# A two-layer transformer trunk with routed experts: expert rows added to the residual by accumulating DMAs, the last two experts' rows spread by matmul in both layers, and a closing norm that works by rows

## Chip, cores, metric

The kernel runs on one core of a Trainium2 chip. The metric is the device time of one execution in microseconds. All arithmetic is in 32-bit floats; large products are made of three matmuls over numbers split into a rounded hi part and a lo rest (float32r).

## What is computed

400 token rows of width 1024 (16 meta rows, 256 prompt rows, 8 x 16 decode rows) go through two layers. What matters here is the second half of a layer, after attention:

```python
probs = softmax(x @ router_w)                     # 16 experts in 4 groups
# per token: the best group, the two best experts inside it
gate = probs[chosen two]; gate = gate / sum(gate)
for e in range(16):
    hid = silu(x @ w_gate[e]) * (x @ w_up[e])     # 1024 -> 512
    y = y + combine[:, e] * (hid @ w_down[e])     # combine holds the gates
x = layer_norm(ALPHA * x + y, ln2_g, ln2_b)
```

The result of layer 0 is the input of the next layer's projection (w_in, 2048 columns). The result of layer 1, without the meta rows, is the output.

## The kernel before

**Data.** H holds the residual as rows, four tiles of 128 (tile 3 has the 16 meta rows; layer 1's experts work on tiles 0 to 2 only). FT holds it transposed for the projections, as hi (FThi) and lo (FTlo). ring has six slots of 2 MB for weights, filled by SP's DMAs in a fixed order.

**Experts.** Routing gives each token two seats, (expert, place). POOL gathers up to 128 rows of an expert from the copy xs in DRAM with an indirect DMA (L2131), PE transposes them, and PE multiplies with the gate and up weights (`up`, L930) and with the down weights (`down`, L963). ACT rounds each quarter of the weights (L1810, L1823), DVE subtracts for the lo part (L1342, L1349). Experts go in eight pairs. The result (up to 128 x 1024 in PSUM) is copied by ACT or, for the last but one expert, by DVE into ob (L1840, L1369), and POOL scatters it to the buffer ys in DRAM (L2181), at row token + 400 * k for the token's choice k. PE's order for a pair is written out in `pair` (L1004), ACT's at L1849 and DVE's at L1393. Should an expert have more than 128 tokens, further rounds follow; with these inputs there is one round per layer.

**Gates.** POOL computes each tile's two gates (`share`, L2134), for the last tile after the first gathers and after the residual has been multiplied by ALPHA (`h_prepared`, L2050). PE counts the tokens of each expert (`totals`, L588) at the end of the routing.

**End of layer 0.** All sixteen experts scatter. POOL waits for the scatters (round_closed), then ACT loads both halves of ys for each tile (L2003) and multiplies the first by its gate (`scale_y`, L1655), POOL or DVE adds it to H (`y_summed`, L2057; L1579), DVE multiplies and adds the second (L1583) and takes mean and variance (`ln_front`, L1077). POOL takes the power for rstd (L2047), DVE writes normalized rows z (`ln_z`, L1086), PE transposes them (L555), ACT and DVE apply gain and bias per partition while copying to FT (`turned_h`), ACT rounds (L1643), POOL subtracts (`ft_rest`, L2071). PE's projection in layer 1 starts once all four tiles are rounded (L797). DVE applies gain and bias to the rows in H afterwards (L1104, L1110). SP's loads of w_in into slots 3 and 2 wait until ys has been read; those into slots 0 and 1 don't.

**End of layer 1.** Experts 14 and 15 are not scattered. DVE builds for each a matrix seat x token that holds the gates (`end_gates`, `end_seats`), PE transposes it (L990), ACT copies it to spread, and PE multiplies it in full 32-bit passes with the two results (`end_sums`, L993). The rows of experts 0 to 13 are loaded from ys by SP as soon as expert 13's scatter has landed (L512 to L515), ACT scales the first half between its weight splits (`end_scaled`, L1843), POOL adds it (L2063), DVE the second half (L1442) and PE's sums (L1448). The norm follows by rows, on DVE, ACT and POOL; SP stores each tile (L532).

```python
                if seated and l == END:
                    act.wait_ge(spread_ps, 1)
                    act.activation(spread, PS[:, 2:4, ...], ACT.Copy).then_inc(spread_sb, 1)
                    end_scaled(0)
                split_down(PAIRS - 1, 1, range(1), last=True)
```

## Time and profile before

| | |
|---|---|
| runs, us | 1056.26, 1053.43, 1056.66; median 1056.26 |
| profiled execution, span | 1056.7 us, 15062 instructions |
| PE, DVE, ACT, POOL busy | 91%, 81%, 62%, 26% |
| granted clock, mean | 0.946 |
| DMA | 272.26 MB, mean 258 GB/s |

The profile gives no time for the profiled execution beside its span; the span lies 0.4 us above the median of the runs. Layer 0's experts run from about 215 to 510 us and layer 1's from about 733 to 1031; the attention of each layer lies before them. The time of an instruction is its busy time on its engine. A line can be that of a helper with several callers. In the timeline an engine with a q behind its name (SPq, ACTq) is its queue issuing a DMA.

### The profile page before, as it was taken

How to read it: one execution, taken by the hardware profiler on the slowest of the kernel's cores; microseconds unless marked ns; L12 is line 12 of the kernel's file. 1: busy time of each engine (PE TensorE's matmuls, PEld its weight loads, DVE VectorE, ACT ScalarE, POOL GpSimd, SP SyncE). 2: the span in 40 equal slices, each digit the busy share in tenths (PEclk: the TensorE clock that was granted, in tenths of full speed). 3: DMA queues.
4: the chain of work that ended last, by engine and by line, in shares of the span. 5: the costliest groups of instructions: out<-in, count | busy, mean ns of one | idle time of the engine just before them, and what ended most of it. 6: DMA issues, size and time to landing. Idle time of an engine off the chain costs nothing. (4 is left out here: it accounts for less than half of the span.)

```text
span 1056.7 us, 15062 instructions
## 1 busy us (share of the span) xinstructions
PE 964.3 (91%) x5040; PEld 791.6 (75%) x5040; DVE 858.3 (81%) x1216; ACT 658.1 (62%) x939; POOL 276.6 (26%) x322
## 2 busy tenths in 40 slices
PE   4999889989999999999349998898899999999984
PEld 4988667767888888888239886687688888888861
DVE  8867657879999898989596676487899898998997
ACT  5355431357888888888444455214788888888871
POOL 1223532434111111100171235323511111111033
PEclk9999889889999999999759998896999999999997
DMA  9423610689999999996660336217999999999761
GB/s 353 171 103 124 240 63 21 228 326 322 370 363 367 368 356 357 374 365 262 228 206 24 104 123 223 80 48 292 347 361 370 368 357 368 371 364 371 259 245 62
DMA packets 116829, 272.26 MB, mean 258 GB/s; under 512 B 8749, under 2 KB 11045, under 8 KB 116750
## 3 DMA queue, kind: packets, MB, share of 16 engines
q1 hardware_dynamic: 98512, 235.94, 61.6%
q10 hardware_dynamic: 8718, 20.28, 5.5%
q0 software_dynamic: 9536, 15.26, 3.9%
q8 instruction: 31, 0.51, 0.2%
q14 instruction: 32, 0.26, 0.1%
HBM read 266.51 MB, written 24.87 MB: 276 GB/s over the span
## 5 line engine op out<-in xcount | busy, mean ns | idle before, releaser
L1342 DVE TENSOR_TENSOR w_lo<-ring,w_hi 128x1024 fp32r<-128x1024 f32 x256 | 303.9, 1239 | 38.8 <-ACT w_hi L1810 36.4
L1810 ACT ACTIVATE w_hi<-ring 128x1024 fp32r<-128x1024 f32 x256 | 261.0, 1060 | 50.8 <-PE PS L982 27.0
L945 PE MATMUL PS<-w_hi,x_hi 128*128 128x512 f32 x512 | 164.0, 402 | 3.0 <-ACT w_hi L1810 3.0
L950 PE MATMUL PS<-w_lo,x_hi 128*128 128x512 f32 x512 | 162.5, 399 | 3.1 <-DVE w_lo L1342 3.0
L1349 DVE TENSOR_TENSOR w_lo<-ring,w_hi 128x1024 fp32r<-128x1024 f32 x128 | 159.0, 1248 | 6.7 <-ACT w_hi L1823 5.0
L945 PE MATMUL PS<-w_hi,x_lo 128*128 128x512 f32 x512 | 160.5, 394 | 0.3 <-DVE x_lo L1332 0.3
L1823 ACT ACTIVATE w_hi<-ring 128x1024 fp32r<-128x1024 f32 x128 | 135.2, 1058 | 29.3 <-PE PS L950 28.6
L2131 POOL DMA_INDIRECT M<-xs,idx x30 | 52.6, 1755 | 255.3 <-PE PS L926 226.9
L950 PEld LDWEIGHTS PS<-w_lo,x_hi 128*128 128x128 f32 x512 | 95.7, 188 | 28.3 <-DVE w_lo L1342 6.6
L945 PEld LDWEIGHTS PS<-w_hi,x_lo 128*128 128x128 f32 x512 | 96.6, 189 | 23.5 <-DVE x_lo L1332 0.8
L945 PEld LDWEIGHTS PS<-w_hi,x_hi 128*128 128x128 f32 x512 | 94.4, 189 | 24.1 <-issue 1.8
L2181 POOL DMA_INDIRECT ys<-M,idx x30 | 30.4, 1012 | 224.4 <-ACT M L1840 207.8
L978 PE MATMUL PS<-w_hi,h_hi 128*128 128x512 f32 x240 | 78.0, 406 | 0.0
L982 PE MATMUL PS<-w_lo,h_hi 128*128 128x512 f32 x240 | 75.4, 395 | 0.0
L978 PE MATMUL PS<-w_hi,h_lo 128*128 128x512 f32 x240 | 75.0, 394 | 0.0
L615 PE MATMUL PS<-FThi,wp_hi 128*128 128x400 f32 (+2 forms) x264 | 56.9, 360 | 7.0 <-ACT FThi L1643 6.6
L555 PE MATMUL PS<-CT,N 128*128 128x128 f32 (+1 forms) x120 | 21.9, 342 | 45.0 <-DVE N L1093 44.9
L1138 DVE TENSOR_TENSOR w_lo<-ring,wp_hi 128x1024 fp32r<-128x1024 f32 x32 | 39.7, 1250 | 26.1 <-ACT wp_hi L1653 25.8
L1633 ACT ACTIVATE FT<-PS,CT 128x128 f32<-128x128 f32 (+1 forms) x68 | 24.0, 443 | 57.2 <-PE PS L555 57.2
L555 PEld LDWEIGHTS PS<-CT,N 128*128 128x128 f32 (+1 forms) x120 | 17.7, 189 | 50.2 <-DVE N L1093 40.8
L1741 ACT ACTIVATE N<-N 128x144 f32<-128x144 f32 (+2 forms) x48 | 22.8, 475 | 51.3 <-DVE N L1167 51.3
L615 PEld LDWEIGHTS PS<-FThi,wp_hi 128*128 128x128 f32 x264 | 47.7, 197 | 8.9 <-ACT FThi L1643 7.3
(247 smaller groups left out, 1750.6 us busy)
## 6 DMA issues: line engine op xcount, KB each, us to landing
ring<-in_w_gate SPq DMA_DIRECT2D x32, 2048.0 KB, 15.6
ring<-in_w_up SPq DMA_DIRECT2D x32, 2048.0 KB
ring<-in_w_down SPq DMA_DIRECT2D x32, 2048.0 KB, 15.1
ring<-in_w_in SPq DMA_DIRECT2D x8, 2048.0 KB, 13.0
ring<-in_w_out SPq DMA_DIRECT2D x4, 2048.0 KB, 7.8
M<-in_cache_k ACTq DMA_DIRECT2D x8, 512.0 KB, 3.3
M<-in_cache_v ACTq DMA_DIRECT2D x8, 512.0 KB, 5.4
xs<-H POOLq DMA_DIRECT2D x6, 512.0 KB, 5.5
```

Source lines behind the costliest of these rows:

```text
L555: mm = pe.transpose(PS[:, bank, at:at + TN[j]], z[0:TN[j], k * P:(k + 1) * P], ident[0:TN[j], 0:TN[j]])
L615: mm = pe.matmul(PS[:, n % 2, c], a[:, k, :], b[:, k, c], start=(start and k == 0), stop=(stop and k == KT - 1))
L945: pe.matmul(PS[:, n, :], x[:, c:c + P], w_hi[j][:, k * 512:(k + 1) * 512], start=(j == 0 and k == 0 and x is x_hi[par]), stop=False)
L950: mm = pe.matmul(PS[:, n, :], x_hi[par][:, c:c + P], lo[:, k * 512:(k + 1) * 512], start=False, stop=(j == 3 and k == 1))
L978: pe.matmul(PS[:, bank + half, :], h[:, c], w_hi[j][:, half * 512:(half + 1) * 512], start=(j == 0 and h is hidden[0]), stop=False)
L982: mm = pe.matmul(PS[:, bank + half, :], hidden[0][:, c], lo[:, half * 512:(half + 1) * 512], start=False, stop=(j == 3))
L1138: dve.tensor_tensor(lo, w, wp(n).bitcast(F32), ALU.subtract).then_inc(wp_lo_done, 1)
L1342: dve.tensor_tensor(lo, w, w_hi[j][:, :].bitcast(F32), ALU.subtract).then_inc(up_lo, 1)
L1349: dve.tensor_tensor(lo, w, w_hi[j][:, :].bitcast(F32), ALU.subtract).then_inc(down_lo, 1)
L1810: act.activation(w_hi[j][:, :], quarter(3 * par + n, j)[0], ACT.Copy).then_inc(up_hi, 1)
L1823: act.activation(w_hi[j][:, :], quarter(5 if par == 0 else 2, j)[0], ACT.Copy).then_inc(down_hi, 1)
L2131: pool.indirect_dma_start(xg[e % 2], None, xs, bass.IndirectOffsetOnAxis(ap=idx[:, 0, e:e + 1], axis=0), bounds_check=last_row, oob_is_err ...
```

## The change

1. Each scattered row is multiplied by its gate before it leaves. PE sums the gates by seat (`share_part`, from the one-hot seats and the new share_rows, which POOL writes at the end of `share`), in the middle of expert 0's up-projection, where `totals` now stands too. DVE copies the sums to seat_gate, and the copies to ob scale by it. POOL's last `share` comes before the wait for the index.
2. There is a buffer ys for each layer, cleared at the start by DMAs from SP out of a block of zeros.
3. Once expert 13's scatter has landed, POOL adds ys to H by DMAs with accumulation, first choice 0 of every tile, then choice 1 of each tile when its first has landed (`results_added`). SP's loads of w_in for slots 1, 3 and 2 wait for all of them.
4. In both layers experts 14 and 15 stay on the chip: the seat matrix holds ones, ACT rounds the gated result (`end_rounded`), DVE takes the rest (`end_rest`), and PE multiplies both with spread in single float32r passes (`end_sum`).
5. The closing norm is the same in both layers and works by rows: DVE adds PE's sum and takes the row sum in one instruction, ACT squares with the negative mean as bias and sums, POOL scales and takes the power, DVE applies the gain and, a tile later, rstd and bias. In layer 0, PE then transposes the finished rows of H, ACT rounds them from PSUM to FThi and DVE subtracts for FTlo (`turned_rest`). Tile order in layer 0 is 0, 1, 3, 2. The projection of layer 1 starts as that of layer 0 does (`first_two`), with the columns of the first three tiles.

The core of the diff (declarations and the code for further rounds left out):

```diff
@@ SP
-                    if l > 0 and s == 3:
+                    if l > 0 and s == 1:
                         for j in range(4):
-                            sp.wait_ge(y_in[j], 16 * l)
+                            sp.wait_ge(y_in[j], 32 * l)
...
                     load(s, t["w_out"][l, :, 512 * half:512 * half + 512].rearrange("(k p) n -> p k n", p=P))
+                    if l == 0:
+                        if half == 0:
+                            sp.wait_ge(zeros_set, 1)
+                        sp.dma_start(ys[half][0:768, :].rearrange("(a p) n -> p a n", p=64),
+                                     zeros.unsqueeze(1).broadcast_to([64, 12, D])).then_inc(ys_zero, 16)
+                        sp.dma_start(ys[half][768:2 * NTOK, :], zeros[0:32]).then_inc(ys_zero, 16)
@@ PE
+            def turn_h(l, n):
+                j = order(LN2[l])[n]
+                pe.wait_ge(h_done, ln_count(LN2[l], n))
+                if n == 2:
+                    pe.wait_ge(ft_hi, 4 * (l + 1) + 1)
+                    pe.wait_ge(ft_lo[l + 1], 1)
+                for k in range(KT):
+                    mm = pe.transpose(PS[:, TURN_BANKS[n][k // 4], k % 4 * P:k % 4 * P + TN[j]],
+                                      H[0:TN[j], j, k * P:(k + 1) * P], ident[0:TN[j], 0:TN[j]])
+                mm.then_inc(h_turned, 1)
...
+                        if n == 0 and first and seated:
+                            totals(l)
+                            for m in range(len(order(LN1[l]))):
+                                pe.wait_ge(shared, 4 * l + m + 1)
+                                mm = share_part(l, m, 5)
+                            mm.then_inc(share_ps, 1)
...
                 def end_sums():
+                    pe.wait_ge(spread_sb, l + 1)
+                    pe.wait_ge(o_sb, 16 * rb + 15)
+                    end_sum(0, 0)
+                    end_sum(1, 0)
+                    end_sum(0, 1)
+                    end_sum(1, 1)
+                    pe.wait_ge(o_sb, 16 * rb + 16)
+                    for n in range(2, len(order(LN2[l]))):
+                        if n == 3:
+                            pe.wait_ge(first_kept, 1)
+                        end_sum(n, 0)
+                        end_sum(n, 1)
@@ DVE
+            def mean_taken(l, n):
...
+                c = did(sum_added(l, n, st[:, 12:13]))
+                after(c)
+                dve.sem_inc(first_kept if n == 0 else comb, 1)
+                dve.tensor_scalar(st[:, 13:14], st[:, 12:13], -1.0 / D, None, ALU.mult).then_inc(mean_done, 1)
...
+                for n in range(last + 1):
+                    mean_taken(l, n)
+                    if n >= 1:
+                        shifted(l, n - 1, gain_at[n - 1])
+                    if n >= 2 and l + 1 < DEPTH:
+                        turned_rest(l, n - 2)
+                    gain_at.append(gained(l, n))
                 if l + 1 < DEPTH:
+                    w_split(l + 1, 0)
+                shifted(l, last, gain_at[last])
+                if l + 1 < DEPTH:
+                    turned_rest(l, last - 1)
+                    w_split(l + 1, 1)
+                    turned_rest(l, last)
+                    w_split(l + 1, 2)
+                    w_split(l + 1, 3)
@@ ACT
+                    act.activation(ob[par].rearrange("p (b n) -> p b n", b=2), PS[:, bank:bank + 2, :], ACT.Copy,
+                                   scale=seat_gate[:, bass.ds(2 * i + par, 1)]).then_inc(o_sb, 1)
...
+                for n in range(len(tiles_of(l))):
+                    squared_rows(l, n)
+                    if l + 1 < DEPTH and n >= 2:
+                        turned_hi(l, n - 2)
@@ POOL
+            def results_added(l):
                 pool.wait_ge(h_scaled, l + 1)
+                for k in range(2):
+                    for j in order(LN2[l]):
+                        if k == 1:
+                            pool.wait_ge(y_in[j], 32 * l + 16)
+                        pool.dma_start(H[0:TN[j], j, :], result_rows(l, k, j), accum_op=ALU.add).then_inc(y_in[j], 16)
...
-                    pool.wait_ge(shared, 4 * l + len(order(LN1[l])) - 1)
-                    share(l, len(order(LN1[l])) - 1)
+                    pool.wait_ge(ys_zero, 64)
...
                 rows_out(l, len(tiles) - 1)
+                share(l, len(tiles) - 1)
                 pool.wait_ge(xg_zero, l + 1)
```

## Rows read from the trace of the kernel before

**Rows 1.** The page, part 1: busy time, share of the span, instructions of each engine.

```profile
PE 964.3 (91%) x5040; PEld 791.6 (75%) x5040; DVE 858.3 (81%) x1216; ACT 658.1 (62%) x939; POOL 276.6 (26%) x322
```

**Rows 2.** Stretches (start:end, length), busy us (instructions), granted clock, DMA share, GB/s.

```profile
72.00:114.00 42.00, 42.00 (x325) 37.47 (x324) 30.82 (x73) 22.98 (x61) 15.49 (x32) 1.00 0.32 109
255.00:292.00 37.00, 37.00 (x173) 30.23 (x172) 33.37 (x31) 31.11 (x34) 6.59 (x5) 1.00 1.01 366
488.00:504.00 16.00, 16.00 (x72) 12.97 (x71) 13.27 (x13) 13.69 (x16) 0.98 (x1) 1.00 1.00 372
510.00:551.00 41.00, 7.17 (x34) 5.71 (x33) 29.31 (x39) 19.54 (x36) 18.86 (x10) 0.54 0.62 219
562.00:680.00 118.00, 113.17 (x753) 96.80 (x751) 69.60 (x155) 56.32 (x141) 40.88 (x71) 0.93 0.31 108
1012.00:1020.00 8.00, 8.00 (x42) 6.57 (x41) 6.30 (x7) 6.47 (x7) 1.63 (x1) 1.00 0.83 319
```

**Rows 3.** Timeline, end of layer 0: start us, length us, engine, line, what, xcount, idle before.

```profile
489.82 0.98 POOL L2181 DMA_INDIRECT ys<-M,idx  x1 [17.03 <-ACT M L1840]
...
501.88 0.60 ACT L1833 ACTIVATE h_hi_end<-PS 128x512 fp32r<-128x512 f32 x1 [0.70 <-PE PS L960]
...
509.60 0.63 PE L982 MATMUL PS<-w_lo,h_hi_end 128*128 128x512 f32 x2
...
515.79 0.93 ACTq L2003 DMA_DIRECT2D M<-ys  x2
...
538.63 1.97 PE L555 MATMUL PS<-CT,N 128*128 128x128 f32 x8 [1.98 <-DVE N L1093]
...
550.93 3.04 PE L615 MATMUL PS<-FThi,wp_hi 128*128 128x400 f32 x8 [4.95 <-ACT FThi L1643]
...
560.44 1.62 PE L615 MATMUL PS<-FTlo,wp_hi 128*128 128x400 f32 x8
```

**Rows 4.** The chain that ended last: start us, length us, what.

```profile
1006.05 6.02 DMA ys<-M,idx
...
1012.63 7.43 DMA ring<-ys
...
1048.68 3.24 DVE H L1598
```

**Rows 5.** Timeline, end of the program.

```profile
1019.07 0.57 ACT L1833 ACTIVATE h_hi_end<-PS 128x512 fp32r<-128x512 f32 x1
...
1030.34 0.63 PE L982 MATMUL PS<-w_lo,h_hi_end 128*128 128x512 f32 x2
...
1040.89 1.29 DVE L1104 SCALAR_TENSOR_TENSOR H<-H,stats,ring 128x1024 f32<-128x1024 f32 x1
```

**Rows 6.** Groups by line and shape: busy us, mean ns, idle before.

```profile
L2131 POOL DMA_INDIRECT M<-xs,idx x30 | 52.6, 1755 | 255.3 <-PE PS L926 226.9 <-DVE idx L1297 24.6 <-issue 3.8
...
L2181 POOL DMA_INDIRECT ys<-M,idx x30 | 30.4, 1012 | 224.4 <-ACT M L1840 207.8 <-DVE M L1369 16.6
...
L1138 DVE TENSOR_TENSOR w_lo<-ring,wp_hi 128x1024 fp32r<-128x1024 f32 x32 | 39.7, 1250 | 26.1 <-ACT wp_hi L1653 25.8
...
L1362 DVE TENSOR_TENSOR h_lo<-PS,h_hi 128x512 fp32r<-128x512 f32 x30 | 20.7, 691 | 3.7
...
L2047 POOL TENSOR_TENSOR stats<-stats,CT 128x1 f32<-128x1 f32 x15 | 13.2, 877 | 62.4 <-DVE stats L1084 62.4
...
L1741 ACT ACTIVATION_READ_ACCUMULATOR N<-N 128x1 f32 x48 | 8.9, 186 | 0.0
...
L1448 DVE TENSOR_TENSOR H<-H,PS 128x1024 f32<-128x1024 f32 x3 | 3.7, 1221 | 1.4 <-PE PS L999 1.3 <-DVE H L1104 0.2
...
L1846 ACT ACTIVATE ring<-ring,N 128x1024 f32<-128x1024 f32 x3 | 3.4, 1145 | 0.9 <-DMA ring<-ys 0.9
```

**Rows 7.** DMA issues: out<-in, engine, xcount, KB each, median us to landing.

```profile
xs<-H POOLq DMA_DIRECT2D x6, 512.0 KB, 5.5
...
ys<-M,idx POOLq DMA_INDIRECT x30, 7.8
```

**Rows 8.** Timeline, start of the experts of layer 1.

```profile
731.70 0.98 PE L602 MATMUL PS<-N 128*128 128x32 f32 x8
...
732.51 0.82 PE L593 MATMUL PS<-N,CT 128*128 128x16 f32 x6
```

More of the change, by code:

```diff
@@ L416, in program, with sum_count, scattered_count, result_rows @@
         LN2 = [2, 4]
-        DVE_TURNS = [4, 4, 2, 4]
+        TURNED = [0, 4, 8, 8]
+        DVE_TURNS = 4
+        def sum_count(l, n):
+            return sum(len(order(LN2[m])) for m in range(l)) + n + 1
+        def scattered_count(l, r, seated):
+            return 16 * (PAIRS * r - l - (0 if seated else 1))
+        def result_rows(l, k, j):
+            return ys[l][NTOK * k + P * j:NTOK * k + P * j + TN[j], :]
         def turned_at(q, n, k):
-            if q == LN2[0]:
-                d = DVE_TURNS[q]
-                first = 2 + 3 * (n % 2)
-                return (first, k * P) if k < d else (first + 1 + (k - d) // 4, (k - d) % 4 * P)
             if q in LN1:
@@ L604, in index_part, with share_part @@
                 return mm
+            def share_part(l, n, bank):
+                tiles = order(LN1[l])
+                j = tiles[n]
+                for k in range(2):
+                    mm = pe.matmul(PS[:, bank, 2 * NE:3 * NE], hot[k][0:TN[j], j, :], share_rows[0:TN[j], j, k, :],
+                                   start=(n == 0 and k == 0), stop=(n == len(tiles) - 1 and k == 1))
+                return mm
             def task_bank(l, i):
@@ L1010, in pair @@
                     up(i, 1, False)
-                    if last and seated and l == END:
+                    if last and seated:
                         seats_turned()
@@ L1324, in reseat @@
                 index(rb, r, 7)
+                shares(rb, r, 7)
             def moe_round(l, rb, r, seated):
@@ L1393, in pair @@
                 def pair(i, first, last):
-                    ending = last and seated and l == END
+                    ending = last and seated
                     if not first:
@@ new lines, in turned_rest @@
+            def turned_rest(l, n):
+                j = order(LN2[l])[n]
+                c = slice(TC[j], TC[j] + TN[j])
+                dve.wait_ge(ft_hi, 4 * (l + 1) + n + 1)
+                for half, bank in enumerate(TURN_BANKS[n]):
+                    k = slice(4 * half, 4 * half + 4)
+                    last = dve.tensor_tensor(FTlo[:, k, c], PS[:, bank, :].rearrange("p (k n) -> p k n", k=4)[:, :, 0:TN[j]],
+                                             FThi[:, k, c].bitcast(F32), ALU.subtract)
+                last.then_inc(ft_lo[l + 1], 1)
@@ L2176, in moe_round @@
                         gather(e + 4)
-                    if first and l == END and e + 2 >= NE:
+                    if first and e + 2 >= NE:
                         continue
```

488 lines of the change are left out of this document (218 added, 270 removed).

## The prediction

> **What bounds the kernel now.** I read the page first. PE is busy for 91% of the span and DVE for 81% [rows 1], which says little before the stages are told apart. In an expert stretch PE has no idle time (37.00 of 37.00 us), with DVE at 33.4 and ACT at 31.1, and the DMA engines full at 366 GB/s [rows 2]: PE sets the pace, and anything put into its order there lengthens the program. The attention of layer 1 has PE at 113 of 118 us. Two places are different. Between the layers, 510 to 551, PE works 7.2 of 41 us and has the lower of its two clock levels for most of it (0.54 granted) while DVE works 29.3 [rows 2]. The other is the end. So I went through the order of time at these two. In layer 0 the last down-projection matmul ends at 510.23 (call it T), the first projection of layer 1 starts at 550.93 and its first two chunks are done at 562.06 [rows 3]: 51.8 us. At the end T is 1030.97 [rows 5] and the span 1056.7, so 25.7 us. The chain of waits there goes through DMAs: the scatter of expert 13's rows, 6.02 us, and the loading back of rows, 7.43 [rows 4]. ACT scales those rows between its weight splits, and the splits come late: from h_hi_end to T takes 11.90 us in layer 1 [rows 5] and 8.35 in layer 0, where nothing is scaled there [rows 3].
>
> **Start of the experts (both layers): +4.3.** The count of tokens (totals) moves from ahead of expert 0 to the middle of its up-projection, and the share sums are new in PE's order. Four index products took 0.98 us and three totals 0.82 [rows 8]. The share sums are eight such products in layer 0 and six in layer 1, so 1.96 and 1.47. In layer 1 the totals stood beside a wait for x_lo, so all of their 0.8 now counts; in layer 0 they stood in the path before, and I count nothing. Sum 2.0 + 2.3. Nothing hides it, as everything after stands in PE's order; if the little idle time after the first up-projection took it in, it would be 0. On POOL the last tile's shares now come before its wait for the index. They are a dozen small operations, and while they run the second gather can come about a microsecond later in layer 0; its rows are wanted only behind the up-projection of expert 0. SP's load of expert 1's down weights waits for that gather and moves as much. DVE gets one copy of 128x16.
>
> **Expert stretches: 0.** The gate is now a per-partition scale of the copy to the output buffer, on ACT. A scaled ACT copy of 128x1024 takes 1.145 us [rows 6], about 0.1 over an unscaled one; 31.1 of 37 us leaves room for that.
>
> **Clearing the result buffers: 0.** Two buffers of 3.28 MB each are written by SP, behind the two w_out loads of layer 0. At 372 GB/s that is 17.6 us of the DMA engines in a stretch in which they are 0.32 busy [rows 2]. In SP's order the second w_out half stands behind the first clearing and the first expert loads behind the second; both wait for PE's projections first. If the clearing ran at half that rate it would still fit.
>
> **Last pair of layer 0: +1.3.** The seats of experts 14 and 15 are now built and transposed in layer 0 too. In layer 1, which has them, the time from the scatter's issue to h_hi_end is 13.02 us (1006.05 to 1019.07) and in layer 0 12.06 (489.82 to 501.88) [rows 3 to 5]. The difference, 0.96, for six transposes becomes 1.3 for eight.
>
> **From T to the end of a sum (both layers).** Experts 14 and 15 no longer scatter. After T: ACT rounds the gated rows of expert 15 (1.15), DVE takes the rest (1.22), PE adds two products (0.5): the sum of the first tile stands at T + 3.1 with its hand-overs. Expert 14 and the hi part of 15 are done beside this.
>
> **New norm, layer 1: -8.0 with the splits.** ACT waits for no DMA now, so h_hi_end to T takes 8.35 instead of 11.90: -3.5. Then DVE goes, per tile: sum from PSUM 1.22 [rows 6], the small mean 0.35 with its wait, shift of the tile before 1.29, gain 1.29 [rows 5]; 4.2 us. The third tile's gain ends at T + 14.5; its rstd (ACT square 1.15 + 0.19, POOL's small step and power 0.88 [rows 6]) at about 14.9, its shift at 16.3. The store then takes what it took before, 1051.92 to 1056.7, 4.8. That is T + 21.2 against T + 25.7: -4.5. The heavy POOL additions that stretch DVE's last operation to 3.24 us [rows 4] are gone.
>
> **New norm, layer 0: -11.4.** The same loop with four tiles, plus the transposed rows. The third round waits for ACT (square until T + 13.2, two copies of 128x512 at 0.6 as in [rows 3]), so DVE's first rest (2 x 0.69 [rows 6]) ends at 15.9; gain 17.2, fourth mean 18.8, shift 20.1, the second rest, again behind ACT, 22.8, gain 24.1, weight split (1.25 [rows 6]) 25.4, last shift 26.7. PE turns that tile in 1.97 us [rows 3] and starts projecting at T + 28.8. The two chunks took 11.1 us before; 24 further narrow matmuls and no wait give 11.6, so T + 40.4 against 51.8. The residual rows no longer have to be finished behind the projection. ACT's loads of the caches and the state come later than the norm but earlier in the program than now.
>
> **The accumulating DMAs: 0, bounds 0 and +40.** No row shows one. In layer 0 POOL can start them at 489.82 + 7.8 = 497.6 [rows 3, 7], and the rows of the first tile are complete after 2.16 MB of 3.28; they are wanted at T + 3.1 = 514.6 with T at 511.5. That asks for some 127 GB/s. In layer 1 the start is at 1012.07 [rows 4], T at 1027.4, the first tile needs 2.1 MB by 1030.5 and the third 3.15 MB by about 1039: 117 GB/s. Plain loads ran at 319 and 372 GB/s [rows 2]. An accumulate also reads its destination, so twice the bytes are read; I take half, 160 GB/s, and it is hidden. The cover is thin, and the far bound is one DMA after the other at the landing time of POOL's own rows, 5.5 or 7.8 us for 512 KB or less [rows 7], 95 or 67 GB/s. SP's loads of w_in for slots 1, 3 and 2 are queued behind these DMAs; 6 MB at 372 GB/s takes 17 us from about 519, and slot 1 (landed at about 525) is first wanted for the fifth chunk, behind T + 40.4 = 551.9.
>
> **Sum:** +2.0 +2.3 +1.3 -11.4 -8.0 = -13.8. The profiled execution's span is 1056.7 us, 0.4 above the median of the three runs (1056.26), and I predict against it: 1042.9 us.
>
> **Rivals.**
> - *Late accumulates (slower side).* POOL's DMAs are served in turn at 5.5 us each. At 95 GB/s the second tile of layer 0 is complete at 525.9 instead of the 517.7 at which DVE wants it, +8, and the third of layer 1 at T + 17.7 instead of 10.8, +7: 1058. At 7.8 us each it is +20 and +21: 1084. It decides below about 125 GB/s and turns the change into a loss below 97. For it: thin cover, no row of the kind. Against it: at 255 to 292 the queues together moved 366 GB/s [rows 2] with POOL's transfers among them. Chance 0.12, of which 0.09 lie slower than before.
> - *POOL's issues are held by DVE.* A gather's issue takes 1.755 us on average and a scatter's 1.012 [rows 6]; DVE is splitting weights while the accumulates are issued. Eight issues each held 0.75 us make +6 by the last and +4 by the first tile's second; the cover takes 3 of it in layer 0, so +1 to +3 per layer, and as much again in the power steps of the norm: 1048. Chance 0.2. The Trainium skill (SBUF — State Buffer, Who interferes with whom) says that a DVE copy or tensor_scalar in a two-port mode locks GpSimd out for the whole instruction, and that DMAs issued from GpSimd then stall while their descriptors are written. Most DVE work in the window is a subtraction of two tensors, for which the page infers no such stall, so by the page alone this rival would give about 1044; the 1.755 in the row speaks against so clean a split.
> - *The start of the experts costs nothing* (PE idles there a little) and the norm goes as computed: 1038.6. Chance 0.13.
> - *ACT's scaled copies reach PE in the expert stretches*: 28 of them by 0.1 us, +2.8, 1045.7. Chance 0.1.
> - *The change does only the end's part*, the layer boundary being held by the loads of w_in that now wait for the accumulates, or by the caches: -8.0 and +5.6, so 1054.3. Chance 0.05.
>
> **How the numbers follow.** The forecast as it stands has 0.4. A measurement of this kernel tells 0.3%, about 3 us, from no change. The range of 1036 to 1055 takes in the forecast with an error of 2 us in each norm, the held issues, the scaled copies and the free start, some 0.85 in all, and leaves out the late accumulates. Faster by over 0.3% (below 1053): 0.87; same: 0.04; slower: 0.09.
>
> **What would show it.** Right: no scatter after expert 13's, DVE's first sum 3 us after the last down matmul in both layers, with no wait for a DMA in front of it; first projection 29 us after T; span end 21 us after T; h_hi_end to T near 8.4 in both layers; PE idle nowhere new between experts. Wrong: a wait of DVE for H from POOL's queue before the sums (late accumulates), issues of POOL's direct DMAs over 1.2 us each (held), a gap of PE at the first copies of an expert, or a start of expert 0's n = 1 half less than 1.5 us later than now. The prediction falls if the accumulates move less than 120 GB/s.

## The result, and the profile after

The changed kernel takes 1044.78 us (median of 4 executions, 1043.86 to 1046.99) against 1056.46 for the kernel before; the ratio is 0.9889, with a 95% interval of 0.9871 to 0.9908. The prediction was 1042.9 with a range of 1036 to 1055: faster, as forecast, and 1.9 us less so. The profiled execution has a span of 1042.5 us. Every execution's time is 1.8 us above its span (the profiled one took 1044.27), which the prediction left out when it set the span of before beside the median of the times; the profiled execution of before was in truth about 2 us slower than its median. So the two profiles differ by 14.2 us and the medians by 11.7.

The total hides several misses that cancel. To see them I cut both traces at the same five marks: T0 and T1 are the ends of the last down-projection matmul of each layer; the marks between are SP's issues in layer 1 of the first w_out load, of the first expert's gate load, and of the next gate load. Each of these issues waits for a buffer that earlier work sets free, so each stands for the progress of that work.

| stage | before | after | change | predicted |
|---|---|---|---|---|
| start to T0 | 510.23 | 514.53 | +4.30 | +3.3 |
| T0 to w_out issue | 84.61 | 75.29 | -9.32 | -11.4 |
| to first expert load issue | 50.68 | 50.64 | 0 | 0 |
| to next expert load issue | 63.68 | 59.86 | -3.82 | 0 |
| to T1 | 321.77 | 319.20 | -2.57 | -1.2 |
| T1 to end | 25.73 | 22.98 | -2.75 | -4.5 |
| sum | 1056.7 | 1042.5 | -14.2 | -13.8 |

First the page, part 1, of the changed kernel, to be set beside [rows 1].

```profile
PE 969.9 (93%) x5132; PEld 800.2 (77%) x5132; DVE 833.4 (80%) x1206; ACT 654.1 (63%) x927; POOL 253.7 (24%) x337
```

Then two stretches of it, with the columns of [rows 2].

```profile
255.00:292.00 37.00, 37.00 (x176) 30.23 (x175) 34.01 (x32) 30.51 (x34) 5.88 (x4) 1.00 1.01 364
510.00:551.00 41.00, 24.89 (x115) 20.23 (x114) 28.49 (x37) 14.35 (x23) 7.66 (x12) 0.71 0.83 246
```

The expert stretch is as it was: PE has no idle time in 37 us, ACT's scaled copies fit in beside it. Between the layers PE now works 24.9 of 41 us where it worked 7.2 [rows 2], because the projections start inside the window.

The timeline at the end of layer 0 (answers to [rows 3]; columns as there) shows the new norm, engine by engine.

```profile
514.62 1.12 ACT L1924 ACTIVATE ob_hi<-PS,N 128x1024 fp32r<-128x1024 f32 x1 [3.60 <-PE PS L1011]
520.96 2.95 ACT L1716 ACTIVATE wp_hi<-ring 128x1024 fp32r<-128x1024 f32 x3 [5.21 <-issue]
523.82 1.13 ACT L1725 ACTIVATE M<-H,stats 128x1024 f32<-128x1024 f32 x1
...
515.77 1.28 DVE L1424 SCALAR_TENSOR_TENSOR x_lo<-PS,N,ob_hi 128x1024 fp32r<-128x1024 f32 x1 [2.56 <-ACT ob_hi L1924]
518.69 1.23 DVE L1505 SCALAR_TENSOR_TENSOR H<-PS,H 128x1024 f32<-128x1024 f32 x1 [1.63 <-DMA H<-ys]
...
526.08 1.28 DVE L1533 SCALAR_TENSOR_TENSOR H<-N,stats,M 128x1024 f32<-128x1024 f32 x1 [2.99 <-POOL stats L2120]
...
532.25 1.29 DVE L1543 TENSOR_TENSOR FTlo<-PS,FThi 128x512 fp32r<-128x512 f32 x2 [1.01 <-ACT FThi L1734]
...
538.45 1.29 DVE L1543 TENSOR_TENSOR FTlo<-PS,FThi 128x512 fp32r<-128x512 f32 x2 [1.05 <-ACT FThi L1734]
...
543.32 1.97 PE L575 MATMUL PS<-CT,H 128*128 128x128 f32 x8 [4.83 <-DVE H L1533]
544.93 2.16 PE L644 MATMUL PS<-FThi,wp_hi 128*128 128x272 f32 x8
```

The mean of the first tile is ready at 520.3, but ACT, which must square the centred row, has done nothing since 515.7: it stands idle for 5.21 us "until issue", that is, for nothing that the profile names, and then does three weight roundings first. The square comes at 523.82, GpSimd's power after it, and DVE waits 2.99 us for that at its first shift. Ahead of this DVE waits 1.63 us for an accumulating DMA. The two waits of about 1 us for ACT's copies were in the prediction.

The end of the program (answers to [rows 5]) has the same hole in ACT.

```profile
1011.16 0.60 ACT L1909 ACTIVATE h_hi_end<-PS 128x512 fp32r<-128x512 f32 x1 [0.77 <-PE PS L989]
...
1019.55 1.12 ACT L1924 ACTIVATE ob_hi<-PS,N 128x1024 fp32r<-128x1024 f32 x1 [3.54 <-PE PS L1011]
1026.36 1.15 ACT L1725 ACTIVATE M<-H,stats 128x1024 f32<-128x1024 f32 x1 [5.68 <-issue]
...
1023.05 1.22 DVE L1505 SCALAR_TENSOR_TENSOR H<-PS,H 128x1024 f32<-128x1024 f32 x1 [1.06 <-PE PS L1029]
...
1028.63 1.29 DVE L1533 SCALAR_TENSOR_TENSOR H<-N,stats,M 128x1024 f32<-128x1024 f32 x1 [0.99 <-POOL stats L2120]
```

Here no DMA is waited for: the sum's wait is for PE. From h_hi_end to T1 it is 8.36 us instead of the 11.90 of [rows 5]. And the chain that ended last has no DMA in it behind expert 13's scatter, where [rows 4] had two. ACT's hole stands in this chain in both layers, first with all of its length and then with 1.75 us.

```profile
515.61 5.23 issue
...
1024.61 1.75 issue
```

The start of the experts of layer 0, on PE:

```profile
220.90 0.62 PE L973 MATMUL PS<-w_lo,x_hi 128*128 128x512 f32 x2
221.37 1.05 PE L613 MATMUL PS<-N,CT 128*128 128x16 f32 x8
222.35 2.06 PE L631 MATMUL PS<-N 128*128 128x16 f32 x16
224.34 0.89 PE L968 MATMUL PS<-w_hi,x_hi 128*128 128x512 f32 x2
225.02 1.05 PE L968 MATMUL PS<-w_hi,x_lo 128*128 128x512 f32 x2
```

The narrow matmuls take 3.0 us. What was not foreseen is behind them: two matmuls of 128x512 take 0.62 ahead of them and 0.89 to 1.05 behind them, until 228. In 220 to 240 the granted clock is 0.91 where it was 1.00 in the kernel before.

Four questions follow: what holds ACT, what the clock did in the third stage of the table, what the start of the experts really costs, and what the accumulation itself costs.

### The profile page after: what moved, and what is told of

Its sections match the earlier page's. It is cut to its first block, busy times and chain, and to the rows that moved or that the text cites. A ratio compares the mean times of both kernels' runs of the same rounds, so it can differ in the third digit from the quotient of the medians.

```text
span 1042.5 us, 15247 instructions
## 1 busy us (share of the span) xinstructions
PE 969.9 (93%) x5132; PEld 800.2 (77%) x5132; DVE 833.4 (80%) x1206; ACT 654.1 (63%) x927; POOL 253.7 (24%) x337
## 4 chain that ended last, share of the span: by engine, by line
PE 80%; DVE 13%; issue 3%; ACT 2%; POOL 1%; DMA 0%; ACTq 0%; DVEq 0%; POOLq 0%
PE PS L968 22%; PE PS L644 12%; PE PS L1007 11%; PE PS L973 11%; PE PS L1011 6%; PE PS L949 3%; PE PS L815 1%; PE PS L816 1%; PE PS L817 1%; PE PS L989 1%; DVE w_lo L1391 1%; DVE stats L1128 1%; PE PS L587 1%; DVE N L1140 1%; DVE w_lo L1182 1%
## 5 line engine op out<-in xcount | busy, mean ns | idle before, releaser
L1391 DVE TENSOR_TENSOR w_lo<-ring,w_hi 128x1024 fp32r<-128x1024 f32 x256 | 303.6, 1236 | 41.5 <-ACT w_hi L1886 39.0
L1398 DVE TENSOR_TENSOR w_lo<-ring,w_hi 128x1024 fp32r<-128x1024 f32 x128 | 154.4, 1220 | 4.3 <-ACT w_hi L1899 4.3
L2241 POOL DMA_INDIRECT ys<-M,idx x28 | 28.1, 1004 | 208.6 <-ACT M L1918 208.6
L644 PE MATMUL PS<-FThi,w_lo 128*128 128x400 f32 (+2 forms) x272 | 55.0, 346 | 0.0
L1007 PEld LDWEIGHTS PS<-w_hi,h_lo 128*128 128x128 f32 x240 | 45.0, 188 | 11.0
L644 PE MATMUL PS<-FTlo,wp_hi 128*128 128x400 f32 (+2 forms) x272 | 53.3, 340 | 0.0
L1011 PEld LDWEIGHTS PS<-w_lo,h_hi 128*128 128x128 f32 x240 | 45.0, 188 | 10.4
```

What stands on the lines that cost most here:

```text
L644: mm = pe.matmul(PS[:, n % 2, c], a[:, k, :], b[:, k, c], start=(start and k == 0), stop=(stop and k == KT - 1))
L1007: pe.matmul(PS[:, bank + half, :], h[:, c], w_hi[j][:, half * 512:(half + 1) * 512], start=(j == 0 and h is hidden[0]), stop=False)
L1011: mm = pe.matmul(PS[:, bank + half, :], hidden[0][:, c], lo[:, half * 512:(half + 1) * 512], start=False, stop=(j == 3))
L1391: dve.tensor_tensor(lo, w, w_hi[j][:, :].bitcast(F32), ALU.subtract).then_inc(up_lo, 1)
L1398: dve.tensor_tensor(lo, w, w_hi[j][:, :].bitcast(F32), ALU.subtract).then_inc(down_lo, 1)
```

## The experiments

All figures are medians; the interval is that of the ratio to the kernel before, measured beside it. The stretches are read from one profiled execution of each kernel.

**Both kernels again.** These two came first, to see how far one profile can be trusted.

> The kernel before, once more. In the first pair of profiles the granted clock of the layer 1 attention differed (661 to 677 us: 0.77, 0.50, 0.50, 0.95 before; 1.00 after, in the same work), and the expert weights' issue stood 5.1 us earlier after. Theory A, the clock is chance and differs from execution to execution: this profile shows other clocks in 661 to 677, and a span that moves by 3 to 4 us with them. Theory B, it belongs to the kernel: again about 0.50 for some 10 us there, span 1050 to 1055.

> The changed kernel, once more. Theory A (chance): some executions have the low clock in the layer 1 attention and give about 1048 where the first profile gave 1044.3. Theory B (the clock follows from where the work stands against the throttle's windows, and so belongs to the kernel): again 1.00 in 656 to 672 us, 1044 to 1046, ratio 0.987 to 0.991.

Before: 1057.92, against its own other executions 1.0017 (1.0004 to 1.0031), so that even an interval that leaves out 1 can be 0.2% of nothing. After: 1044.9, ratio 0.9906 (0.9879 to 0.9933). The stage from one expert load to the next took 63.66 us before and 59.87 after: the same 3.8 us as in the first pair, as theory B has it. The repeat of after is 3.5 us shorter than its first profile (span 1039.0) with the same code: T0 is 1.0 earlier, and the stage up to T1, 317.15 us, is 2.0 shorter, with a granted clock of 0.62 to 1.00 in 712 to 728 where it was 0.50 to 0.69. That a single pair of profiles agrees with a sum to 0.4 us says little for the sum.

**What holds ACT.** At this place ACT loads the number of further expert rounds into a register (zero, with this data), and branches over them.

```
-                more = act.value_load(more_rounds[0:1, 0:1], min_val=0, max_val=3)
-                R = more + 1
-                with act.If(more > 0):
-                    with act.Fori(1, R) as r:
-                        moe_round(l, rb, r, False)
-                rb = rb + R
+                rb = rb + 1
```

> The changed kernel without the load of the number of further rounds, the branch and the further rounds on ScalarE alone (they are never entered with this data). Theory 1, what holds ScalarE for 5.2 us (layer 0) and 5.7 us (layer 1) between its last expert result and the closing norm is this load and branch: the gap falls to what the data wait leaves, the first square stands at about T + 6.5 in layer 0 (after the three weight roundings, 515.7 to 518.6, and the mean at 520.3) instead of T + 9.3, VectorE's 2.99 us wait for GpSimd's power goes, the span falls by 3 us in layer 0 and by 1.8 us in layer 1: about 1040, ratio to before 0.984. Theory 2, the gap is another wait that the profile does not name: the gap stays, 1044 to 1045.

```
                 with act.If(more > 0):
-                    with act.Fori(1, R) as r:
-                        moe_round(l, rb, r, False)
+                    act.wait_ge(routed, l + 1)
```

> The changed kernel with ScalarE's load and branch kept, but the body of the branch cut to one wait, so that the jump is over two instructions instead of about 258. Theory 1a, the jump over far code costs the time: as without load and branch, about 1040, gap under 1.5 us. Theory 1b, the load of the number into a register (with its two following instructions) or the branch itself costs it: the gap stays near 5 us, 1044 to 1045. In between, the gap shows the two shares.

Without the branch: 1039.64, ratio 0.9850 (0.9834 to 0.9867). Its T0 to w_out's issue is 70.24 us instead of 75.29 and its T1 to the end 21.7 instead of 23.0, so that layer 0 gave 5.1 us where 3 were expected and layer 1 1.2 where 1.8 were. With the short body: 1038.98, ratio 0.9829 (0.9808 to 0.9850). The timeline of ACT with the short body:

```profile
514.84 1.12 ACT L1924 ACTIVATE ob_hi<-PS,N 128x1024 fp32r<-128x1024 f32 x1 [3.60 <-PE PS L1011]
516.16 2.95 ACT L1716 ACTIVATE wp_hi<-ring 128x1024 fp32r<-128x1024 f32 x3 [0.20 <-issue]
520.47 1.16 ACT L1725 ACTIVATE M<-H,stats 128x1024 f32<-128x1024 f32 x1 [1.36 <-DVE stats L1515]
```

The load, its register instructions and the branch stand in this kernel as before and take 0.20 us. So neither the load nor the branch costs the 5.2 us, but the jump over some 258 instructions that were never run. What the engine waits for there the DMA queues show. The kernel's code comes in through two queues of kind "instruction", 8 and 14. The DMA view of the changed kernel has (packets, MB, share of 16 engines), first for 515.8 to 519.0, the first three microseconds of the hole, in which the accumulating DMAs' queue is the only one with packets, and then for 519.0 to 520.9 its instruction queue:

```profile
q0 software_dynamic: 202, 0.68, 109.7%
```

```profile
q14 instruction: 2, 0.02, 3.5%
```

So for more than 3 us no code comes in beside the accumulating DMAs, then two packets of it do, and at 520.96 ACT goes on. The profile doesn't say for which engine a packet of code is. How much the full engines matter the plain loads will show.

**The same cut in the kernel before.**

> The kernel before with ScalarE's further rounds cut to one wait, the same cut that took 5.7 us off the changed kernel. Theory 1 (before, the jump stood beside the wait for the last scatters and their loads, so that it cost nothing): 1055 to 1058, ratio 0.998 to 1.001, and the gap of 4.45 us between the last result and the loads' issue is filled by the wait for the scatter. Rival (the loads of the rows were issued late by the jump, and the kernel before paid for it too): the loads are issued 2 to 4 us earlier in layer 0 and the run is 1.5 to 4 us shorter, 1052 to 1055.

1055.38, ratio 0.9984 (0.9966 to 1.0003). ACT's timeline in it:

```profile
510.06 1.02 ACT L1840 ACTIVATE M<-PS 128x1024 f32<-128x1024 f32 x1 [4.58 <-PE PS L982]
515.14 0.98 ACTq L2002 DMA_DIRECT2D M<-ys  x2
```

The kernel before has its last result here, and its loads at 515.79 [rows 3]:

```profile
510.32 1.02 ACT L1840 ACTIVATE M<-PS 128x1024 f32<-128x1024 f32 x1 [4.58 <-PE PS L982]
```

From the end of the last result to the loads 4.06 us are left of 4.45, now without a long jump: that wait was for the last scatter. The jump stood beside it and cost 0.4 us of it at most; the change took the scatter away and left the jump bare.

**The jump moved to where ACT waits anyway.** A whole kernel again, with its further rounds:

```
+                with act.If(more < 1):
+                    closing(rb + 1)
                 with act.If(more > 0):
                     with act.Fori(1, R) as r:
                         moe_round(l, rb, r, False)
+                    closing(rb + R)
```

`closing` holds the weight roundings, the squares and the copies of tiles 0 and 1.

> The changed kernel, whole, with ScalarE's jump moved: the closing norm's squares, roundings and the first two tiles' copies stand inline in a body that is entered when there are no further rounds, and the jump over the further rounds comes after them, in the 6.5 us in which ScalarE waits for the last transposes (in layer 1 after its last square). Theory 1 (a jump over far code holds ScalarE for some 5 us, wherever it stands; with a two-instruction body the gap was 0.20): the gap before the roundings falls to under 1 us in both layers, the 5 us show up before the copies of tiles 2 and 3, where they are covered but for at most 1 us; 1039 to 1041, ratio 0.983 to 0.986, as with the short body (0.9829). Rival: the second test and jump cost as much as they save, 1043 to 1045.

1035.89, ratio 0.9815 (0.9788 to 0.9842): the median lies 3 us below the range of theory 1, the ratio is that of the short body within the intervals. ACT:

```profile
514.69 2.96 ACT L1716 ACTIVATE wp_hi<-ring 128x1024 fp32r<-128x1024 f32 x3
518.82 1.15 ACT L1725 ACTIVATE M<-H,stats 128x1024 f32<-128x1024 f32 x1 [1.18 <-DVE stats L1515]
...
537.14 0.34 ACT L1734 ACTIVATE FThi<-PS 128x64 fp32r<-128x64 f32 x2 [3.22 <-issue]
540.83 0.60 ACT L1734 ACTIVATE FThi<-PS 128x512 fp32r<-128x512 f32 x1 [3.35 <-PE PS L575]
```

The hole before the roundings is gone. It stands at 533.9, with 3.22 us, in front of a copy of 16 columns, and the copy that matters still waits for PE. From T0 to the first projection it is 26.95 us instead of 30.40, and from T1 to the end 21.7 instead of 23.0: against the prediction's 28.8 and 21.2. In layer 0 this is 1.9 us below it.

**The accumulation.** `accum_op=ALU.add` is taken off the loads, so that they overwrite the rows and the addition is left out.

> The changed kernel with the eight and six accumulating DMAs made plain loads into the same residual rows: it leaves out the addition, so that the rows are overwritten. Theory 1 (the accumulation costs nothing on the path but VectorE's wait of 1.4 to 1.6 us for the first tile in layer 0, and a plain load lands sooner): landing median under the 8.6 us of the accumulating ones, VectorE's wait 0 to 1 us, and, as ScalarE's jump sets the pace behind it, 1043.5 to 1045, ratio 0.988 to 0.991. Rival (accumulating DMAs slow the expert weights' loads or each other): landing falls to half or less and the last pair of layer 0 gets shorter by over 1 us, under 1042.5.

1046.11, ratio 0.9905 (0.9878 to 0.9933), above theory 1's range in time and inside it by the ratio. The queue's own answers, first of the changed kernel, then of this one:

```profile
L2129 POOL DMA_DIRECT2D H<-ys x14: 856/983/1899, 501.2 to 1017.1; - x14
...
DMA to landing us min/median/max: 5.7/8.2/13.2
```

```profile
L2129 POOL DMA_DIRECT2D H<-ys x14: 499/538/601, 500.4 to 1015.8; - x14
...
DMA to landing us min/median/max: 4.0/5.4/9.6
```

Durations are minimum, median and maximum in ns. An accumulating issue holds GpSimd 0.98 us instead of 0.54 and lands 2.8 us later. T0 stayed (513.57 against 514.53 and 513.52), so they take nothing from the experts. Behind T0 the first sum has no wait for a DMA, and the first projection comes at T0 + 28.17 instead of 30.40. A part of that is ACT's hole, which here is 2.50 us instead of 5.21, though its code is the changed kernel's. One stretch of 1 us inside the hole, first of the changed kernel and then of this one, shows what differs: the DMA engines are full in the one (share 1.15) and empty in the other (0.04).

```profile
518.00:519.00 1.00, 1.00 (x6) 0.57 (x5) 0.31 (x1) 0.00 (x0) 0.00 (x0) 1.00 1.15 209
```

```profile
516.00:517.00 1.00, 0.84 (x4) 0.72 (x5) 0.18 (x2) 0.00 (x0) 0.00 (x0) 1.00 0.04 8
```

And the code comes at once. In 514.8 to 516.1, right behind ACT's last result at 514.78, the instruction queue has:

```profile
q14 instruction: 2, 0.02, 4.0%
```

So the jump waits for code that comes by DMA behind the rows: 2.5 us with the engines nearly empty, 5.2 with them full. With the short body, which leaves 0.20 us, this is shown from two sides. The Trainium skill (Runtime: NRT & Kernel Launch, Instruction fetch mechanics) has the rule: most engines hold two pages of 256 instructions, and a taken branch to outside of them makes the engine fetch the target page by DMA before it can go on. The trace agrees, with 0.20 us for the near jump and 2.5 to 5.7 for the far one, and with the two packets of code ahead of its end; the page gives no time. DVE's jump at the same point is over about 200 instructions instead of 258, and its hole is short: its first sum here starts 0.82 us after x_lo, released by PE. That would fit the rule too, but no run moved it. The time of the whole did not follow, since 63.66 us instead of 59.86 went by between the two expert loads: the clock again.

**The moment of the clock.** Ahead of the last shift of layer 0, DVE makes 3.5 idle passes.

```
+                    dve.wait_ge(h_done, ln_count(LN2[l], last - 1))
+                    for width in (1024, 1024, 1024, 512):
+                        x = free[:, 0:width]
+                        then(dve.scalar_tensor_tensor(x, x, 1.0, x, ALU.mult, ALU.mult))
```

> The changed kernel with four idle passes on VectorE (3.5 x 1.28 us and their waits, about 5.0 us) ahead of the last tile's shift in layer 0, so that layer 1 begins where it began in the kernel before (5.0 us later than in the changed one). Theory P (the low clock at 661 to 675 us in both profiles of before, 1.00 in all four of the changed kernel and its variants, follows from the moment at which the attention's work falls): the clock falls to 0.5 again there for some 10 us, and the run is 8 to 10 us longer, 1053 to 1055, ratio 0.997 to 0.999. Theory K (it follows from something else that the change did, not from the moment): clock 1.00 there, 1049 to 1050, ratio 0.993 to 0.994.

1052.12 (1046.39 to 1057.08), ratio 0.9952 (0.9922 to 0.9983): 7.3 us above after as measured first, 5 to 7 by the ratios. That lies between theory K's 5 and theory P's 8 to 10, and the interval takes in both, so the time doesn't decide; the trace has to. The delay itself came to 4.1 us in T0 to w_out's issue (79.39 against 75.29). Stretches, with the columns of [rows 2], of the kernel before, of this one, and of after at the same work:

```profile
650.00:682.00 32.00, 29.32 (x161) 21.40 (x162) 16.20 (x35) 12.71 (x34) 11.92 (x14) 0.74 0.43 157
```

```profile
650.00:682.00 32.00, 28.89 (x159) 21.11 (x160) 16.24 (x35) 12.97 (x34) 11.85 (x15) 0.74 0.44 159
```

```profile
645.00:677.00 32.00, 27.89 (x172) 20.64 (x172) 18.29 (x36) 13.30 (x36) 15.42 (x17) 0.90 0.52 187
```

With the start of before, this execution has the clock of before: 0.74 on average, with 0.50 (the lower level, 1.2 GHz) from 664 to 672, and 63.69 us for the stage. But the delay doesn't settle it for every execution. Three of the ten took 1046.4 to 1047.4, with 0.964 to 0.965 as the mean clock of the whole, the other seven 1051.2 to 1057.1 with 0.945 to 0.957. The three are 4 us or more below the rest and look like theory K's course; they were not profiled. Nor is it as simple as early and late. norm_order below starts layer 1 twelve microseconds earlier than before and has the low stretch too; the plain loads have it with w_out issued at 586.29, and the short body has not, at 586.89:

```profile
636.00:668.00 32.00, 27.02 (x151) 19.61 (x152) 16.33 (x38) 13.11 (x34) 13.03 (x17) 0.73 0.46 170
```

```profile
636.00:668.00 32.00, 27.36 (x173) 20.01 (x172) 18.45 (x42) 14.22 (x37) 15.84 (x21) 0.89 0.52 190
```

The upper one is norm_order, the lower closing_first, whose instructions in this stretch are the same. In fourteen profiles the stage takes either 63.7 to 64.3 us (seven) or 59.3 to 59.9 (seven), nothing between. PE does much the same before both: 3.4 of 5 us busy at 660 in the kernel before, where the clock then fell, and 3.4 of 5 at 655 in the changed one, where it did not. What tips it stays open, and so does whether chance takes part in it.

**The price of the start.** The totals and share sums move behind the transposes of expert 0's hidden rows, where PE waited for ACT.

```
                         mm.then_inc(up_used, 1)
-                        if n == 0 and first and seated:
-                            totals(l)
-                            ...
@@
                     turn_hid(i, 0, first)
+                    if first and seated:
+                        totals(l)
+                        ...
                     up(i, 1, False)
```

> The changed kernel with TensorE's totals (8 matmuls) and share sums (16) moved from between the two halves of the first expert's up projection to behind the transposes of its hidden rows, where TensorE waited 1.58 us for ScalarE and then 0.65 and three times 0.3 us for VectorE; VectorE's copy and count move behind the third quarter of the second expert's up half. Theory 1 (the start of the experts costs what these matmuls take on TensorE's path, 3.0 us in layer 0 and 2.0 in layer 1, and the wait there hides most of it): the first transposes come 3.0 and 2.0 us earlier, 1.5 to 3 us and 1 to 2 us of it last: 1040.5 to 1042.5, ratio 0.985 to 0.988. Rival (VectorE is the bound behind the transposes, and its six small operations move onto its path): under 1 us in all, 1044 to 1045. If the granted clock of the first half changes with it, the windows 213 to 233 show it.

1037.78, ratio 0.9826 (0.9801 to 0.9852), 2.7 us below the theory's range; the profiled execution is the slowest of the four (1039.79). PE in layer 0:

```profile
214.01 1.22 PE L968 MATMUL PS<-w_hi,x_hi 128*128 128x512 f32 x2
...
227.66 0.64 PE L973 MATMUL PS<-w_lo,x_hi 128*128 128x512 f32 x2
228.13 1.04 PE L949 MATMUL PS<-CT,M 128*128 128x128 f32 x8
...
229.64 1.06 PE L613 MATMUL PS<-N,CT 128*128 128x16 f32 x8
```

The first up projection takes 14.1 us to the transposes instead of 18.5 (213.05 to 231.57): 3.0 are the narrow matmuls, and 1.4 the full clock that was now kept there. The stretch of low clock is not gone, though: it comes at 233 to 236 here (0.50), again some 3 us behind the narrow matmuls. From the first up matmul to T0 it is 297.23 us against 301.48 and 300.96, so 3.7 to 4.3 of the 4.4 stay. T0 itself comes only 2.3 to 3.3 us earlier (511.24), as the first up matmul starts 1.0 to 1.5 us later than in after's two profiles, behind work that the edit doesn't touch. In layer 1 the comparison with least low clock on both sides is that of norm_order with norm_order_shares below: 317.68 to 315.70 us for the stage up to T1, 2.0.

**Order of the closing norm.** ACT copies tile n - 2 before it squares tile n; DVE's first weight rounding goes behind the last shift.

```
                         if l + 1 < DEPTH and n >= 2:
                             turned_hi(l, n - 2)
+                        squared_rows(l, n)
@@
-                if l + 1 < DEPTH:
-                    w_split(l + 1, 0)
                 shifted(l, last, gain_at[last])
                 if l + 1 < DEPTH:
+                    w_split(l + 1, 0)
                     turned_rest(l, last - 1)
```

> closing_first, and in the closing norm of layer 0 ScalarE copies the turned rows of tile n - 2 before it squares tile n, and VectorE shifts the last tile before it rounds the first projection weights. Theory 1 (VectorE is the bound from the first shift on, and each of its waits there, 1.01 and 1.05 us for ScalarE's copies, and the 1.2 us of weight rounding ahead of the last shift, is on the path): first projection 3.0 to 3.3 us earlier after the last down matmul, two thirds of them at least in the time: 1032.5 to 1034, ratio 0.978 to 0.980. Rival (the square of tile n comes a microsecond late and GpSimd's power with it, so that VectorE waits there instead): under 1 us, 1035 to 1036.

1041.64, ratio 0.9865 (0.9837 to 0.9892): slower than closing_first, outside both ranges. The local part came, smaller than asked: first projection at T0 + 24.84 instead of 26.95, w_out's issue at T0 + 69.32 instead of 70.59. Both waits for ACT's copies are gone, but the first sum waited 1.86 us for its DMA instead of 1.21, and a new wait stands at the last shift:

```profile
518.01 1.22 DVE L1505 SCALAR_TENSOR_TENSOR H<-PS,H 128x1024 f32<-128x1024 f32 x1 [1.86 <-DMA H<-ys]
...
535.50 1.28 DVE L1533 SCALAR_TENSOR_TENSOR H<-N,stats,M 128x1024 f32<-128x1024 f32 x1 [0.52 <-POOL stats L2124]
```

The loss is in the clock: 63.68 us between the expert loads against 59.34, and the stage up to T1 equal (317.68 and 317.66). -1.3 and +4.3 make the 3.1 us between the two spans, 1036.5 and 1033.4. The medians lie further apart, 5.7 us, and the other executions (1036.9 to 1044.3) have no profile.

> norm_order with the totals and share sums behind the first transposes of the hidden rows, as in shares_late. Theory 1 (independent places, so that the gains add: 3.4 us in layer 0 and about 2 in layer 1 by the trace of shares_late): 1027 to 1030, ratio 0.973 to 0.976. Rival (the moment of the layer 1 attention and the start of its experts falls on another stretch of low clock and takes 2 to 4 us back): 1030 to 1033, with the clock of 640 to 725 us to show it.

1028.35 (1027.26 to 1035.19), ratio 0.9750 (0.9722 to 0.9778), as theory 1 had it: the best version here, 16 us under the changed kernel. That is more than the moved code gives, as this profile has the faster course of the clock and norm_order's had the slower. T0 is at 511.75, first projection at T0 + 24.20, the stage between the expert loads 59.34 us.

**Accumulations tile by tile.** The order of issue becomes tile 0, 1, 0 again, 2, 1 again, and so on.

> norm_order_shares with the accumulating loads issued tile by tile (second accumulation of the first tile third in the queue instead of fifth). Theory 1 (the first tile's second accumulation then lands before its sums are done on TensorE, and VectorE's wait of 1.2 to 1.6 us for it in layer 0 goes, as it went with plain loads that landed in 5.4 us): 0.7 to 1.3 us less than norm_order_shares. Rival (the queue is held while GpSimd waits for the first tile, and the last tiles land later than VectorE comes to them): no gain or a loss of up to 2 us, with a wait at the third or fourth sum.

1035.97 (1029.68 to 1038.64), ratio 0.9795 (0.9768 to 0.9823). The profiled execution is the slowest of the six, 10.0 us above that of norm_order_shares. 4.3 us of the loss are once more the clock (63.66 against 59.34), and 4.0 lie in the stage up to T1 (319.73 against 315.70), where the clock was 0.50 from 704 to 724. The edit itself did what theory 1 says at its own place and what the rival says one step further on. DVE:

```profile
514.94 1.22 DVE L1506 SCALAR_TENSOR_TENSOR H<-PS,H 128x1024 f32<-128x1024 f32 x1 [0.82 <-PE PS L1023]
...
520.63 1.28 DVE L1534 SCALAR_TENSOR_TENSOR H<-N,stats,M 128x1024 f32<-128x1024 f32 x1 [1.29 <-POOL stats L2125]
```

and POOL:

```profile
518.33 0.89 POOL L2137 DMA_DIRECT2D H<-ys  x1 [4.45 <-DMA H<-ys]
519.69 0.18 POOL L2124 TENSOR_SCALAR stats<-stats 128x1 f32<-128x1 f32 x1 [0.48 <-issue]
```

The wait of 1.22 us for the DMA at the first sum is gone, but PE's sum is only 0.4 us ahead of where the DMA was, at T0 + 3.34 instead of T0 + 3.75. And GpSimd issues the last accumulation only at 518.33, after waiting for the one before it, and the first tile's power stands behind that in its queue. The wait moved from one cause to the next: T0 to w_out's issue 69.71 us instead of 67.88. These 1.8 us are what the edit itself cost.

## Why the prediction was right, and where it was not

**Faster, by the two closing norms:** shown, with the size in part by luck (see the last point). No scatter stands behind expert 13's, no DMA in the last chain, and DVE's first sum in layer 1 waits for PE.

**Last pair of layer 0, +1.3:** what is left of the shift of h_hi_end (501.88 to 506.16) beside the start is 1.3. Read directly, expert 13's scatter to h_hi_end takes 13.31 us in layer 0 (492.85 to 506.16) instead of 12.06. **h_hi_end to T1, -3.5:** 11.90 to 8.36.

**New norm, layer 0, -11.4:** -9.3. The step that failed is the round of the norm in which ACT was taken as free when the first mean is ready. The sum counted the square from the moment of the mean; measured, it came 3.6 us behind it, as ACT has a jump of its own there, which waits for code while the accumulations fill the DMA engines. The rows of before could not show this: ACT was done at 511.34 and its loads were issued at 515.79 [rows 3], and that gap was the scatter's, as the short body in the kernel before shows. What the scatter hid was not asked. The Trainium skill's rule on far branches (Runtime: NRT & Kernel Launch, Instruction fetch mechanics) spoke against this step and was not weighed; the trace bears it out with 5.21 and 5.68 us. T0 to the first projection is 30.40 us instead of the 28.8 predicted, and 26.95 with the jump moved. So the jump costs 3.5 us there, and the rest of this sum was 1.9 us too long, which hid half of the miss. **New norm, layer 1, -4.5:** -2.75, the same step, 21.7 instead of 21.2 from T1 once the jump is moved.

**Start of the experts, +2.0 and +2.3:** the first transposes came 2.94 us later in layer 0, and taking the matmuls out of the path brought 3.7 to 4.3 there and 2.0 in layer 1. Mis-sized in layer 0: the totals counted in full at their new place, and the matmuls after the narrow ones ran at the lower clock for more than three microseconds. With the -3.5 of layer 1 this makes the stage up to T1 -1.5; it was -2.6 in the first pair and -5.0 in the repeated one (322.14 to 317.15), with different clocks in 700 to 730. What is beyond -1.5 no run separates from the clock.

**Accumulating DMAs, 0:** nearly. All 3.28 MB were in by 524.1, when SP issued the loads that wait for them, 22.9 us after the first issue, so at least 143 GB/s on the average, gaps included, against the 160 that I assumed and the 125 from which lateness decides; while they fill the engines they move 209 GB/s (518 to 519 above), where plain loads moved 366 to 372 [rows 2], so that half was a fair guess. But the sign of late accumulates that the prediction named was there in layer 0: DVE's first sum came at T0 + 4.16 instead of 3.1, behind a wait of 1.63 us for the DMA. The wait was 0.9 to 1.9 us in eight of the ten profiles of kernels that accumulate, and there was none in shares_late and all_four, nor anywhere in layer 1. In the changed kernel the jump covers it; in the improved ones it is on the path.

**The rivals.** Late accumulates: no. Issues held by DVE: an accumulating issue takes 0.98 us and up to 1.90, but a plain one 0.54, at most 0.60, beside the same work of DVE. So what holds it is the accumulation, not DVE. By that, the Trainium skill's inference (SBUF — State Buffer, Who interferes with whom) that subtractions of two tensors do not stall GpSimd's DMAs agrees with the trace. Free start, scaled copies on PE's path, boundary held by w_in: no, by the start's 2.94 us, by 37.00 of 37.00 us of PE, and by projections without a wait for a DMA.

**Clearing the buffers, 0:** no wait shows it; the first up matmul of layer 0 starts at 212.6 to 213.1 in after's two profiles, before 214.9 to 215.7 with the totals ahead of it.

**What was not in the sum:** 3.8 us of clock in the attention of layer 1. It made up for the 3.8 us that the two norms fell short. The forecast was near by luck, for a reason that it did not contain.

## What to carry to other kernels

A wait that ends last hides others beside it on the same path; before a wait is removed, ask of each engine there what it does in that time and whether a hole "until issue" would end earlier. Put the jump over the code of a rare case in front of a long wait, as closing_first does; to place this code so that the common case needs no jump was not tried here. And compare stage by stage: two spans that agree to 0.4 us here were made of five differences of 1 to 4 us.

## What was not expected of the hardware

- A taken branch over about 258 instructions held ACT for 5.0 to 5.7 us where it began with the DMA engines full of accumulating DMAs, 2.50 us with them nearly empty; in front of a long wait, as in closing_first and the three kernels built on it, 3.2 to 4.8 us. Over two instructions, with the register load, 0.20 us. DVE, jumping over about 200 at the same point, lost at most 0.82 us.
- An accumulating DMA into on-chip rows, issued by GpSimd: 0.98 us of issue against 0.54 for a plain one, 8.2 us to landing against 5.4, and about 209 GB/s with the engines full.
- The granted clock between two expert loads of layer 1 takes one of two courses, 4 us apart, in profiles whose instructions there are the same. The profile of a kernel with 4 us of delay had the other course, but its ten executions fall into two groups 4 us apart. Differences of this size between two kernels need this stage looked at before a cause is named.
- 24 narrow matmuls (128x16) in the middle of an up projection were followed by more than 3 us at the lower clock, 1.4 us of time, in all eight profiles that have them there and in none of the three of the kernel before. Behind the transposes they were followed by such a stretch too, in all three profiles.
